# A delta-rule chain in two pairs of heads, its first level by subtraction, in a two-layer hybrid decoder step

## What is computed

```python
G = jnp.cumsum(gc, axis=-1)
decay = jnp.where(incl, jnp.exp(jnp.where(incl, diff, 0.0)), 0.0)
qk = jnp.einsum('nbhid,nbhjd->nbhij', qc, kc) * decay
m = jnp.where(strict, jnp.einsum('nbhid,nbhjd->nbhij', kc, kc) * decay * bc[..., :, None], 0.0)
a = m + jnp.eye(C, dtype=F32)
rhs = jnp.concatenate([vc * bc[..., None], kc * (bc * jnp.exp(G))[..., None]], axis=-1)
sol = lax.linalg.triangular_solve(a, rhs, left_side=True, lower=True, unit_diagonal=True)
...
def step(s, xs):
    w = u_c - kcum_c @ s
    o = qd @ s + qk_c @ w
    s = s * gt + kd.T @ w
```

## Time and profile before

| | us |
|---|---|
| median of 3 runs | 3210.27 (3208.25 to 3211.61) |
| the profiled execution | 3210.03 |
| its span, first to last instruction | 3208.2 |
| PE busy in the span | 2894.5 (90%) |
| DVE, ACT, POOL busy | 1485.8, 1258.8, 812.5 |
| delta stage, layer 1: first L1154 to `kc` of the sample chunk | 705.5 to 943.3 |
| delta stage, layer 2: the same | 2275.6 to 2512.6 |

### The profile page before, as it was taken

The page is one execution under the profiler, slowest core; times in us unless marked ns, Lnnn a source line. Parts: engine busy times, 40 slices in busy tenths (PEclk is TensorE's granted clock), DMA queues, the critical chain, the costliest instruction groups (busy, mean ns, idle before and its releaser), DMA issues. The chain is left out here.

```text
span 3208.2 us, 56817 instructions
## 1 busy us (share of the span) xinstructions
PE 2894.5 (90%) x22582; PEld 2719.8 (85%) x22582; DVE 1485.8 (46%) x2238; ACT 1258.8 (39%) x2255; POOL 812.5 (25%) x364
## 2 busy tenths in 40 slices
PE   4998999989986989999879999899889879899996
PEld 3998988888876979999868989788878769799995
DVE  2362855654433526436136448466444243461541
ACT  3431434751113435345244224367311053552542
POOL 1221222220000424444222213122100024244441
PEclk7998999999975989999979979999999589899998
DMA  5221324533323513232232222254333234123321
GB/s 166 80 83 57 100 88 146 165 104 100 96 67 95 187 53 93 73 106 68 79 96 82 64 79 91 97 183 126 116 90 97 79 121 151 53 81 98 87 83 58
DMA packets 366310, 315.86 MB, mean 98 GB/s; under 512 B 42710, under 2 KB 314488, under 8 KB 365494
## 3 DMA queue, kind: packets, MB, share of 16 engines
q10 hardware_dynamic: 257332, 188.09, 19.7%
q1 hardware_dynamic: 108706, 124.05, 13.1%
HBM read 273.70 MB, written 38.38 MB: 97 GB/s over the span
## 5 line engine op out<-in xcount | busy, mean ns | idle before, releaser
L757 POOL TENSOR_TENSOR w_lo<-w_raw,w_hi 128x1024 fp32r<-128x1024 f32 (+2 forms) x360 | 812.3, 2257 | 2339.0 <-ACT w_hi L1343 2339.0
L764 PE MATMUL big<-uhi,w_hi 128*128 128x272 f32 x3968 | 1208.4, 305 | 62.7 <-DVE ulo L1845 24.4
L766 PE MATMUL big<-uhi,w_lo 128*128 128x272 f32 x3968 | 1165.0, 294 | 0.0
L765 PE MATMUL big<-ulo,w_hi 128*128 128x272 f32 x3968 | 1159.6, 292 | 0.0
L764 PEld LDWEIGHTS big<-uhi,w_hi 128*128 128x128 f32 x3968 | 765.2, 193 | 123.3 <-issue 71.8
L765 PEld LDWEIGHTS big<-ulo,w_hi 128*128 128x128 f32 x3968 | 768.2, 194 | 3.7 <-issue 1.9
L766 PEld LDWEIGHTS big<-uhi,w_lo 128*128 128x128 f32 x3968 | 764.9, 193 | 0.0
L1343 ACT ACTIVATE w_hi<-w_raw 128x1024 fp32r<-128x1024 f32 (+2 forms) x360 | 343.8, 955 | 346.1 <-PE big L766 317.3
L764 PE MATMUL big<-hhi,w_hi 128*128 128x272 f32 x704 | 204.8, 291 | 1.4 <-DVE hlo L2376 1.4
L766 PE MATMUL big<-hhi,w_lo 128*128 128x272 f32 x704 | 203.6, 289 | 0.0
L765 PE MATMUL big<-hlo,w_hi 128*128 128x272 f32 x704 | 202.9, 288 | 0.0
(11 more groups left out here) (351 smaller groups left out, 4111.9 us busy)
## 6 DMA issues: line engine op xcount, KB each, us to landing
w_raw<-in_w_in ACTq DMA_DIRECT2D x66, 1024.0 KB, 5.6
w_raw<-in_w_up ACTq DMA_DIRECT2D x88, 512.0 KB, 5.0
kpage<-in_cache_k SPq DMA_DIRECT2D x128, 256.0 KB, 3.1
w_raw<-in_w_down ACTq DMA_DIRECT2D x32, 704.0 KB, 4.8
d_conv<-in_cache_v SPq DMA_DIRECT2D x64, 256.0 KB, 2.7
d_pad<-in_cache_v SPq DMA_DIRECT2D x64, 256.0 KB, 2.6
gate_dram<-gate_raw ACTq DMA_DIRECT2D x48, 272.0 KB, 2.2
sig<-gate_dram SPq DMA_DIRECT2D x48, 272.0 KB, 3.4
```

The source lines that it names most:

```text
L757: po.tensor_tensor(split_view(lo, t), tile_of(t), split_view(hi, t).bitcast(F32), ALU.subtract).then_inc(w_lo.sem, w_lo.next(t))
L764: pe.matmul(out, wh, xh, start=start, stop=False)
L765: pe.matmul(out, wh, xl, start=False, stop=False)
L766: return pe.matmul(out, wl, xh, start=False, stop=stop)
```

## The change

`d_t` and `d_tt` become one tile `d_T` of two halves, one for heads 0 and 1, one for heads 2 and 3; in each half the T of both heads comes first and then their transposes, so that one DVE instruction updates both. There are two `d_lm` tiles, used in turn. The first level (s = 1) has no matmul of its own: DVE writes I - lm to the transposed part (`first`), PE transposes it (four transposes to X[2]), and ACT copies that to the other part. The six other levels run for each pair of heads on its own: Y in X[2] or X[3], T·Y and its transpose together in X[0] or X[1], the pairs one behind the other. The turn of k (`dkT`) goes from the second level into the head and from X[1] to X[0]. Two more value pages and four more gate steps go into the head (12 in all), two gate steps stand in each of six levels, and the two in the tail (between `do` and `dS`) go. On DVE the two COPYs go, the multiply by `tri` and the ones for `d_kd`, `d_kb`, `d_vb` move behind the first two masks. ACT copies each pair's Y alone, and stores the first gate tile of a chunk behind the first pair's Y of level s = 8.

```diff
-            turn(X[1], ('dvT', c), P, n, [v[:, h, :] for h in range(H)], P)
...
             if c < 4:
                 value_page(next(pages))
                 value_page(next(pages))
-                advance(gates, 8)
...
+            turn(X[1], ('dvT', c), P, n, [v[:, h, :] for h in range(H)], P)
+            if c < 4:
+                value_page(next(pages))
+                value_page(next(pages))
+                advance(gates, 10)
+            turn(X[0], ('dkT', c), P, n, [k[:, h, :] for h in range(H)], P)
+            if c < 4:
+                advance(gates, 2)
+            pe.wait_ge(vec_out.sem, vec_out.at(('first', c)))
+            turn(X[2], ('Y', c, 1), n, n, [one_T(g.d_T, n, h, 1) for h in range(H)], n)
...
+            def level_t(li, hp):
+
+                s, bank = levels[li], X[hp]
+                pe.wait_ge(X[2 + hp].drained, X[2 + hp].at(('Y', c, s, hp)))
+                pe.wait_ge(bank.drained, bank.claim(('T', c, s, hp)))
...
+            for li in range(1, len(levels)):
+                level_y(li, 0)
                 if c < 4:
                     value_page(next(pages))
...
+                if li > 1:
+                    level_t(li - 1, 1)
+                level_t(li, 0)
+                level_y(li, 1)
                 if c < 4:
                     value_page(next(pages))
-                    advance(gates, 1)
+                    advance(gates, 2)
+            level_t(len(levels) - 1, 1)
             if c < 4:
                 advance(gates, 3)
...
-                advance(gates, 2)
                 pe.wait_ge(X[2].drained, X[2].at(('dw', c)))
...
+        def update(c, n, s, hp, last):
+
+            bank = X[hp]
+            ve.wait_ge(bank.filled, bank.at(('T', c, s, hp)))
+            at = 2 * n if last else 0
+            d = g.d_T[0:n, hp, at:4 * n]
+            tt(d, d, bank.ap[0:n, at:4 * n], ALU.subtract).then_inc(bank.drained, 1)
+            ve.wait_ge(bank.drained, bank.at(('T', c, s, hp)))
...
+            block_part(c, n, 0)
+            tt(both(g.d_T, n, 1), ident[0:n, 0:n].unsqueeze(1).unsqueeze(1).to_broadcast([n, 2, 2, n]),
+               g.d_lm[0:n, 0:4 * n].rearrange("p (a h n) -> p a h n", a=2, h=2), ALU.subtract).then_inc(
+                vec_out.sem, vec_out.next(('first', c)))
+            block_part(c, n, 1)
...
+            for li in range(1, len(levels)):
+                if li > 1:
+                    update(c, n, levels[li - 1], 1, False)
+                if li + 1 < len(levels):
+                    block_part(c, n, li + 1)
+                update(c, n, levels[li], 0, li + 1 == len(levels))
+            update(c, n, levels[-1], 1, True)
```

More of the change, by code:

```diff
@@ L384, in allocate @@
             g.s_log = sb("s_log", [P, NEWK], ctx=r2)
-        g.d_dec, g.d_eg, g.d_mt, g.d_lm, g.d_t, g.d_tt, g.d_y, g.d_kd, g.d_vb, g.d_kb, g.d_S = (
-            sb("d_" + n, [P, 512], ctx=r) for n in ("dec", "eg", "mt", "lm", "t", "tt", "y", "kd", "vb", "kb", "S"))
+        g.d_dec, g.d_eg, g.d_mt, g.d_lm, g.d_y, g.d_kd, g.d_vb, g.d_kb, g.d_S, g.d_lm1 = (
+            sb("d_" + n, [P, 512], ctx=r) for n in ("dec", "eg", "mt", "lm", "y", "kd", "vb", "kb", "S", "lm1"))
+        g.d_T = sb("d_T", [P, 2, 512], ctx=r)
     att.close()
@@ new lines, in _, with level_y @@
+            if c < 4:
[7 more added lines that the diff above has]
+            turn(X[2], ('Y', c, 1), n, n, [one_T(g.d_T, n, h, 1) for h in range(H)], n)
+            def level_y(li, hp):
+                s, bank = levels[li], X[2 + hp]
+                lm = (g.d_lm, g.d_lm1)[li % 2]
+                pe.wait_ge(vec_out.sem, vec_out.at(('lm', c, s)))
+                if li == 1:
+                    pe.wait_ge(X[2].drained, X[2].at(('Y', c, 1)))
+                else:
+                    pe.wait_ge(X[hp].drained, X[hp].at(('T', c, levels[li - 1], hp)))
+                pe.wait_ge(bank.drained, bank.claim(('Y', c, s, hp)))
+                for h in range(2):
+                    hs = slice((2 * hp + h) * n, (2 * hp + h + 1) * n)
+                    mm = pe.matmul(bank.ap[0:n, h * n:h * n + n], lm[0:n, hs], one_T(g.d_T, n, 2 * hp + h, 0),
+                                   start=True, stop=True)
+                mm.then_inc(bank.filled, 1)
@@ new lines, in level_t @@
+            def level_t(li, hp):
+                s, bank = levels[li], X[hp]
+                pe.wait_ge(X[2 + hp].drained, X[2 + hp].at(('Y', c, s, hp)))
+                pe.wait_ge(bank.drained, bank.claim(('T', c, s, hp)))
+                for h in range(2):
+                    hs = slice((2 * hp + h) * n, (2 * hp + h + 1) * n)
+                    if s != levels[-1]:
+                        pe.matmul(bank.ap[0:n, h * n:h * n + n], one_T(g.d_T, n, 2 * hp + h, 1), g.d_y[0:n, hs],
+                                  start=True, stop=True)
+                    mm = pe.matmul(bank.ap[0:n, (2 + h) * n:(3 + h) * n], g.d_y[0:n, hs], one_T(g.d_T, n, 2 * hp + h, 1),
+                                   start=True, stop=True)
+                mm.then_inc(bank.filled, 1)
@@ L1205, in _ @@
+            level_t(len(levels) - 1, 1)
             if c < 4:
                 advance(gates, 3)
-            pe.wait_ge(X[0].drained, X[0].at(('YT', c, levels[-1])))
+            for hp in range(2):
+                pe.wait_ge(X[hp].drained, X[hp].at(('T', c, levels[-1], hp)))
             pe.wait_ge(X[1].drained, X[1].claim(('kc', c)))
@@ new lines, in _ @@
+            ve.wait_ge(X[0].filled, X[0].at(('dkT', c)))
+            x = X[0].ap
+            tt(head_view(g.d_kd[0:n, :], P), head_view(x[0:n, :], P), bcast(gEK[0:n, c, :], P), ALU.mult).then_inc(
+                    vec_steps.sem, vec_steps.next())
+            tt(head_view(g.d_kb[0:n, :], P), head_view(x[0:n, :], P), bcast(gBE[0:n, c, :], P), ALU.mult).then_inc(
+                    X[0].drained, 1)
+            ve.wait_ge(X[1].filled, X[1].at(('dvT', c)))
+            tt(head_view(g.d_vb[0:n, :], P), head_view(X[1].ap[0:n, :], P), bcast(gBeta[0:n, c, :], P), ALU.mult).then_inc(
+                    X[1].drained, 1)
```

113 lines of the change are left out of this document (29 added, 84 removed).

## The result

The kernel after takes 3169.43 us (median of four runs, 3168.18 to 3170.81) against 3210.18 for the kernel before beside it: ratio 0.9874, 95% interval 0.9856 to 0.9891. The forecast was 3150, the range 3138 to 3180. So the sign and the range held, but 41 of the forecast 60 us came. A later pair of measurements of the same two kernels gave 3165.66 and 3210.30, 45 us; the four runs of each time (3168.18 to 3170.81, 3163.49 to 3166.42) do not overlap, so medians of two batches can differ by 4 us with the same code.

What follows compares the result with a forecast made beforehand. PE was taken as the bound, busy nine tenths of the span, with waits in the heads. Savings per layer of 18.8 + 5.3 + 2.4 + 3.5 = 30.0 us, 60 in two, gave 3150 from 3210.0; range 3138 to 3180.

Steps and rivals of the forecast that it cites:

- Head: Start of each prompt chunk: without COPYs the wait for `d_eg` goes, head ends at 12.2 us; 18.8 us saved per layer.
- Levels: Second level's Y to `kc`: 27.6 to 27.7 us a chunk against 29.01, saving 5.3 us per layer.
- The missing 0.2 is the copy of Y.: Kernel before, each level: PE's work is 4.41 of 4.63 us, the rest attributed to waiting for ACT's copy of Y.
- 0.05 open: Pair 1's Y waits 1.03 us for DVE's update, with 0.98 of the other pair's products as cover.
- the forecast's 4.45: Level time in us: 0.49 x 2 + 0.98 x 2 + 0.36 x 2 + 0.74 + 0.05.
- Gate store: Once a chunk in the levels: a gate step's 1.14 us wait for its bank's copy goes; mask precedes `w_lo` by 0.5.
- Tail and sample chunk: Tail saves 0.6 us a chunk, 2.4 per layer, with two gate steps moved to the head; sample chunk saves 3.5.
- the shared port: Rival, chance 0.14: in the fourth level DVE's mask comes behind POOL's `w_lo`, waits up to 2.36 us; 20 us lost, 3170.
- The head waits still: Rival, chance 0.14: PE idles in heads or the clock falls, half the pair's cover lost (0.2 a level); 3173 us.
- the slower case: Rival, chance 0.04: new open waits make the clock fall in the levels, up to 210 us more; 3360 us.
- Does less than it says: Rival, chance 0.05: PE is bound in the levels, pairs hide nothing, only the first level goes; 20 us saved, 3190.

Runs made afterwards that it cites:

- e1: Kernel after with the two DVE COPYs of the identity put back at the start of each chunk; 3178.27 us, ratio 0.9898.
- e2: Kernel before with only the two DVE COPYs of the identity moved behind the four TENSOR_SCALARs; 3190.88 us, ratio 0.9935.
- e8: Kernel before with both value pages of a level behind Y, none behind the products for T; 3186.24 us, ratio 0.9925.
- e9: Kernel after with four-head levels, both pages behind Y, last two head gate steps behind T's turn, both s=8 gate steps behind the products; 3126.74 us.
- e10: Kernel after, pairs kept, levels' pages joined by four at s=2, 8, 32, last two head gate steps behind T's turn; 3133.65 us, ratio 0.9765.

## Why the prediction came out as it did

**Head: right, mechanism and size.** 12.2 a chunk and 18.8 a layer were forecast, 12.06 and 18.9 (18.5 by first loads) came. PE waits nowhere for `d_eg`, the clock is 1.00 in chunks 1 to 3, and the one wait left, for the copy of `d_T`, is 0.84 where 0.8 was forecast. e1 and e2 show the cause from both sides: it was the place of the COPYs beside `w_lo`.

**Levels: the term that failed, by 14 us.** Forecast 27.65 a chunk, measured 29.41; the difference is 1.76 a chunk, 14 in eight. It failed at two steps:

- "The missing 0.2 is the copy of Y." The copy was 0.10 of it. The other 0.12 is the edge ahead of a page: a page's first load comes 1.10 behind the first load of Y (788.35 to 789.45), and the sum took 0.98. The pairs don't remove it: pages still stand at two places of a level, both now behind a Y. The edge behind a page, the idle 0.20 ahead of 731.15 in the earlier trace rows, was inside the 0.36 that I took for the page; it was counted, but I read past it as something that could be saved.
- "0.05 open" for pair 1's Y. The cover, the other pair's four products, was taken as 0.98. That is half of the 1.98 for two groups in the earlier trace rows, and the 1.98 holds the edge ahead of the page behind them; without one a group is 0.89, as e8 shows (782.90 to 783.81 is 0.91, 783.81 to 784.70 0.89). And DVE begins 0.38 behind pair 1's products (pair 0's begin to load at 777.91, the update starts at 778.29), not 0.29. The wait is the 0.17 idle ahead of 779.05, and 0.24 by the spacing of loads (777.02 to 779.05 is 2.03, eight products at 0.22 are 1.79).

In the terms of the forecast's 4.45: the two half groups of Y, each ahead of a page, were put at 0.49 and take 0.65 and 0.64, 0.31 more; the products were put at 1.96 and take 1.79, 0.17 less; the open wait is 0.24 for 0.05, 0.19 more. That gives 4.78, and 4.77 was measured. Against the kernel before, the pairs traded a wait of 0.10 for one of 0.24: 4.62 - 0.10 + 0.24 is 4.76. The first level took 3.87 by first loads instead of 3.78, the last 4.76 instead of 4.44.

**Gate store: right.** The wait of 1.14 is gone and the next mask slips in ahead of `w_lo` by 0.4; forecast was 0.5.

**Tail and sample chunk: right, a little low.** Forecast 2.4 and 3.5 a layer; measured 3.0 (0.62 in three chunks, 1.13 in the fourth) and 3.9. By parts: 18.9 - 2.0 + 3.0 + 3.9 = 23.8 a layer against 30.0; the stage of layer 1 went from 237.8 to 214.1, that of layer 2 from 236.8 to 214.1. That is 46.4 in all, 14 short of the forecast 60, and the levels are that shortfall. The rest of the first profile gave 4.2 of it back, that of the second 0.9; this part of the miss is outside the stages, and its cause is open.

That the range held is luck in part. It reached up to 3180 for two rivals, the shared port and heads that still wait, and neither came as a whole; the edge ahead of a page was in none of them.

**Rivals.** The shared port cost PE nothing: all 60 masks took at most 0.692, all ten `first` at most 0.694. But it was near, and in chunk 3 it was a tie. In chunks 1 and 3 of after:

```profile
783.79 0.69 DVE L2188 TENSOR_TENSOR d_lm<-d_mt,consts 128x512 f32<-128x512 f32 x1
...
784.21 2.50 POOL L768 TENSOR_TENSOR w_lo<-w_raw,w_hi 128x1024 fp32r<-128x1024 f32 x1 [21.41 <-ACT w_hi L1370]
...
881.45 0.69 DVE L2188 TENSOR_TENSOR d_lm<-d_mt,consts 128x512 f32<-128x512 f32 x1
...
881.45 1.84 POOL L768 TENSOR_TENSOR w_lo<-w_raw,w_hi 128x512 fp32r<-128x512 f32 x1 [22.54 <-ACT w_hi L1370]
```

In chunk 1 the mask came first by 0.42, and it was `w_lo` that took 2.50 instead of the 2.36 of the earlier trace rows. In chunk 3 both began at 881.45, the mask kept its 0.69, and the shorter `w_lo` took 1.84 instead of the 1.27 of the earlier trace rows. That the later of the two pays is what the Trainium skill says ("SBUF — State Buffer", section "Who interferes with whom"); with e1's COPYs, which came second, the traces agree in both directions. Not quite in size: the Trainium skill has the later one blocked outright, and overlaps of 0.27 and 0.69 cost `w_lo` 0.14 and 0.57, 0.12 to 0.13 less than the overlap. In e9, the fastest kernel, the mask does come second, and pays:

```profile
779.48 2.37 POOL L768 TENSOR_TENSOR w_lo<-w_raw,w_hi 128x1024 fp32r<-128x1024 f32 x1 [21.04 <-ACT w_hi L1356]
...
780.22 2.18 DVE L2172 TENSOR_TENSOR d_lm<-d_mt,consts 128x512 f32<-128x512 f32 x1
783.19 0.69 DVE L2180 TENSOR_TENSOR d_T<-d_T,aux 128x512 f32<-128x512 f32 x1 [0.79 <-PE aux L1196]
```

PE loses nothing by it there: the mask ended at 782.40, the next update had to wait for PE's products until 783.19, and this level is 4.20 (779.87 to 784.07) like its neighbours. So the rival had the delay of a mask about right (1.5 us against up to 2.36), and what a kernel pays for it depends on what stands behind the mask. "The head waits still" was wrong for the head, but its second part, half of the pair's cover lost at 0.2 a level, is what came. The clock stayed at 1.00 in the levels, so the slower case did not come. "Does less than it says" had a true core: with PE bound in the levels the pairs hid nothing, and e9 shows that they need not.

## What to carry to other kernels

Where the busy times of PE's rows leave a small remainder, ask of each idle time what ends it before giving it to the nearest semaphore: a remainder "by issue" at a change of tile size stays when waits are removed, and is cut by joining the groups of that size. Splitting a chain into halves helps only if the other half is longer than the latency it covers; filler at the right place did the same here (e9), and the cheapest half of the gain was one moved block of DVE code (e2). Pull filler together only as far as the places left bare have another cover (e10).

## What the hardware showed unasked

- PE's edges between 128\*128 and 128\*32 matmuls: 0.19 to 0.21 us ahead, 0.20 behind, independent of how many pages stand between (one, two or four).
- A long wait doesn't always bring the clock down. In before, an idle time of 2.91 us between PE's matmuls (the 3.10 of its loads) was followed by 0.50, and in e1 1.93 by a mean of 0.67 over 5.2 us; in e8 the same 2.91 at the same place left it at 1.00. The two waits, before and e8, and the stretch in e8:

```profile
766.15 1.12 PE L826 MATMUL aux<-consts,qkv 128*128 128x128 f32 x4 [2.91 <-ACT d_eg L1343]
...
766.43 0.66 PE L826 MATMUL aux<-consts,qkv 128*128 128x128 f32 x4 [2.91 <-ACT d_eg L1343]
...
759.41:776.79 17.38, 13.27 (x131) 12.11 (x130) 11.48 (x18) 3.21 (x5) 2.35 (x1) 1.00 0.36 107
```

What differs ahead of it is open; the price of a wait in clock is thus not read off its length alone.
